# Laying the weight matrices of a two-block transformer kernel out by chunk, so that each load is contiguous in HBM

## The chip, the cores and the metric

One core of one Trainium2 chip. The metric is device time in microseconds (us) of one launch. TensorE (PE) multiplies, VectorE (DVE), ScalarE (ACT) and GpSimd (POOL) work elementwise, and SyncE (SP) does nothing here but issue DMAs. Two engines issue DMAs: SP issues nearly all of them, ACT a handful.

## The reference

Two blocks follow one another on a sequence of 512 tokens of width 1024, in fp32; all weights are read once.

```
mod = silu(c) @ w_ada + b_ada                      # 1024 x 6144; six vectors of 1024
h = rmsnorm(x) * (1 + sc1) + sh1
proj = h @ w_in                                    # 1024 x 2760
dilated attention (8 heads) + indexed sparse attention (8 heads) -> mixed
x = x + ga1 * (mixed @ w_out)
x = x + ga2 * ((silu(gate) * up) @ w_down)         # gate, up = h2 @ w_gu, 1024 x 5632
x = rmsnorm(x)
# second block
mod = silu(c_2) @ mod_w_2 + mod_b_2                # 1024 x 3072
u = (rmsnorm(x) * (1 + scale) + shift) @ w_in_2    # 1024 x 5120
31-tap depthwise convolution, layernorm, silu, @ pw2_w_2; a linear recurrence beside it
x = x + (1 + gate) * (concat(y_conv, y_lru) @ w_out_2); rmsnorm
```

## The kernel before

Activations stand transposed in SBUF: 128 partitions by 8 slices (k) by 512 tokens. Every fp32 product is made of three products of a rounded part ("hi") and its rest ("lo"): hi by hi, lo by hi, hi by lo.

**Weights** come in chunks of 256 output columns. A chunk is 1024 x 256 values (1 MB) and lands in `w_stage[n % 2]`, 128 partitions by 8 slices by 256 columns. ACT rounds it into `w_hi`, POOL (DVE for the first ones) subtracts into `w_lo`, and PE uses it. SP loads chunk n as soon as `w_lo` of chunk n-2 is made (L474, in `w_dma`). In HBM the matrices stand as the reference has them, row by row, so that a chunk is 1024 pieces of 1 KB. There are 11 chunks of `w_in`, 4 of `w_out`, 22 of `w_gu`, 12 of `w_down`, 20 of `w_in_2`, 4 of `pw2_w_2` and 8 of `w_out_2`.

**Modulation** matrices (`w_ada`, `mod_w_2`) come in 36 chunks of the same size, through L487, L558 and L564 and buffers of their own. The first eight (`ADA_PE`) are multiplied by PE (`ada_rows`, L841) and turned into columns (`ada_turn`, L850); the others by DVE (L2206, L2209).

**The start** is written out by hand. SP issues, in this order: `x` in four parts (L490), two modulation chunks, the first half of `w_in` chunk 0 (L502), `w_in` chunk 1, two more modulation chunks, the other half of chunk 0, four more modulation chunks, and so on. ACT issues four small loads in its own queue: the identity, `c`, `c_2`, and `vrow`, 256 KB of bias and gain vectors (L1382) in 512 pieces of 512 bytes.

PE works strictly in program order. What it does first:

```
for t in range(TT):                       # L866: turn x, slices 0 to 5
pe.wait_ge(s_vec, 16)                     # waits for vrow
                                          # L876: turn vrow; L866 again: slices 6 and 7
pe.wait_ge(s_cact, 1)
ada_rows(0)                               # L841, first modulation chunk
pe.matmul(bank[4][:], ones[:], rstd[:], ...)   # L887
ada_rows(1)                               # L841, second
keep_warm(4, 3); ada_turns(0); keep_warm(14, 3)   # L769, L850
```

`keep_warm` is matmuls whose result nobody reads. Then come, on the first two slices, the first products of `w_in` (`abreast(first, 0, (0, 1))`, L746 to L748), `ada_pair(1)` (modulation chunks three and four, then L850), `abreast` of the second chunk, and so on. The columns that L876 makes of `vrow` are copied by ACT to `vcol` (L1394, L1395); DVE adds them to each modulation vector (L1931).

Of the kernel before, what the change touches and what calls it, by code (L numbers as in the profile page):

```python
# [20 lines left out]
P = 128  # L21
T = 512
TT = T // P
D = 1024
KD = D // P
D_FF = 2816
# [6 lines left out]
NCOL = 256  # L33
# [7 lines left out]
W_IN_COLS = [2304, 2048, 2560, 1536, 1792, 0, 256, 512, 768, 1024, 1280]  # L41
N_IN = len(W_IN_COLS)
C_OUT = N_IN
C_GU = C_OUT + 4
C_DOWN = C_GU + 2 * (D_FF // NCOL)
C_IN2 = C_DOWN + 12
C_LRU = C_IN2 + 20
C_PW2 = C_LRU + 4
C_OUT2 = C_PW2 + 4
# [3 lines left out]
ADA1, ADA2 = 24, 12  # L53
ADA_FIRST, ADA_ATT, ADA_OUT, ADA_LOOP, ADA_DOWN = 8, 16, 20, 24, 35
# [5 lines left out]
ADA_BUF = [0, 2, 5, 7, 1, 4, 6, 8] + [n % 4 for n in range(ADA_ATT - ADA_FIRST)] + [0, 2, 3, 9]  # L60
# [95 lines left out]
def build(nc, a, out):  # L156
    with ExitStack() as ctx:
        offset = [nc.sbuf_base + (-nc.sbuf_base) % 64]

        def fixed(name, shape, dt=F32, at=None):  # L160

            n = 4
            for s in shape[1:]:
                n *= s
            if at is None:
                at = offset[0]
                offset[0] += (n + 63) // 64 * 64
                assert offset[0] <= nc.sbuf_usable_end, (name, offset[0])
            return nc.alloc_sbuf_tensor_at(name, shape, dt, offset=at), at

        def sem(name):
            return ctx.enter_context(nc.semaphore(name))
# [5 lines left out]
        w_stage = [fixed(f"w_stage{b}", [P, KD, NCOL])[0] for b in range(2)]  # L178
# [65 lines left out]
        for b, at in enumerate((at_va, at_ka, at_qb, at_qi, at_score, at_ki, at_pairT, at_qa), start=2):  # L244
            ada_bufs.append(fixed(f"ada_stage{b}", [P, KD, NCOL], at=at)[0])
        ada_stage = [ada_bufs[b] for b in ADA_BUF]
# [9 lines left out]
        ada2_stage, _ = fixed("ada2_stage", [P, KD, NCOL])  # L256
        ada2_acc, _ = fixed("ada2_acc", [P, NCOL])
        late_stage = [ada2_stage] + [fixed(f"late_stage{b}", [P, KD, NCOL], at=(at_hi, at_lo)[b // 2] + (b % 2) * 4 * KD * NCOL)[0]
                                     for b in range(len(ADA_LATE) - 1)]
# [45 lines left out]
        s_stage = [sem(f"w_stage_loaded{b}") for b in range(2)]  # L305
        s_stage0 = sem("first_half_chunk_loaded")
# [7 lines left out]
        s_ada = [sem(f"ada_loaded{b}") for b in range(10)]  # L314
# [4 lines left out]
        s_adaloop = sem("ada_loop_loaded")  # L319
# [125 lines left out]
        def ada_use(c):  # L445

            return ADA_BUF[:c + 1].count(ADA_BUF[c])
# [7 lines left out]
            engine.wait_ge(s_ada[ADA_BUF[c]], 16 * ada_use(c))  # L455


        def w_cols(w, k0, kn, c0):
            return w.rearrange("(k p) c -> p k c", p=P)[:, k0:k0 + kn, bass.ds(c0, NCOL)]


        @block.sync
        def _(sp):
            def w_dma(n, src, half=None):

                b = n % 2 if half is None else half[0]

                if half is None:
                    if n >= 2:
                        sp.wait_ge(s_lo, n - 1)  # L470
                else:
                    sp.wait_ge(s_lo, n - 1)
                kn, cn = src.shape[1], src.shape[2]
                sp.dma_start(w_stage[b][:, 0:kn, 0:cn], src).then_inc(s_stage[b], 16)  # L474

            def ada_dma(c):
                if ada_use(c) > 1:
                    last = max(o for o in range(c) if ADA_BUF[o] == ADA_BUF[c])
                    if last in ADA_PE:
                        sp.wait_ge(s_adadir, ADA_PE.index(last) + 1)  # L480
                    else:
                        sp.wait_ge(s_adaacc, ADA_ORD[last] + 1)
                elif ADA_BUF[c] == 3:
                    sp.wait_ge(s_xt, KD)
                w, j = (a["w_ada"], c) if c < ADA1 else (a["mod_w_2"], c - ADA1)
                src = w.rearrange("(p t) c -> p t c", t=KD)[:, :, j * NCOL:(j + 1) * NCOL]
                sp.dma_start(ada_stage[c][:], src).then_inc(s_ada[ADA_BUF[c]], 16)  # L487

            for t in range(TT):
                sp.dma_start(x_nat[:, t, :], a["x"][t * P:(t + 1) * P, :]).then_inc(s_x[t], 16)  # L490

            def w_in_dma(n):
                c0 = W_IN_COLS[n]
                cn = min(NCOL, a["w_in"].shape[1] - c0)
                w_dma(n, a["w_in"].rearrange("(k p) c -> p k c", p=P)[:, :, c0:c0 + cn])

            ada_dma(ADA_PE[0])
            ada_dma(ADA_PE[1])

            def first_chunk_dma(h):  # L500
                ks = slice(h * KD // 2, (h + 1) * KD // 2)
                sp.dma_start(w_stage[0][:, ks, :], a["w_in"].rearrange("(k p) c -> p k c", p=P)[  # L502
                    :, ks, W_IN_COLS[0]:W_IN_COLS[0] + NCOL]).then_inc((s_stage0, s_stage[0])[h], 16)

            first_chunk_dma(0)
            w_in_dma(1)
            ada_dma(ADA_PE[2])
            ada_dma(ADA_PE[3])
            first_chunk_dma(1)
# [12 lines left out]
            for n in range(N_IN - 4):  # L522
                if ADA_FIRST + 4 + n < ADA_ATT:
                    ada_dma(ADA_FIRST + 4 + n)
                if n == 3:
# [2 lines left out]
                    sp.dma_start(wuk[:], a["w_uk"].rearrange("r (g c) -> r g c", g=4)).then_inc(s_late, 16)  # L528
                    sp.dma_start(wuv[:], a["w_uv"].rearrange("h r d -> r h d")).then_inc(s_late, 16)
                w_in_dma(n + 4)  # L530
            w_dma(C_OUT, w_cols(a["w_out"], 0, KD, 0))
            w_dma(C_OUT + 1, w_cols(a["w_out"], 0, KD, NCOL))
            w_dma(C_OUT + 2, w_cols(a["w_out"], 0, KD, 2 * NCOL))
            w_dma(C_OUT + 3, w_cols(a["w_out"], 0, KD, 3 * NCOL))
            sp.wait_ge(s_pv, 2 * N_A)
            for c in range(ADA_ATT, ADA_OUT):
                ada_dma(c)
# [1 line left out]
            def stream(n0, steps, srcs, first=0):  # L539

                per = len(srcs)
                with sp.Fori(first, first + steps) as j:
                    for q, src in enumerate(srcs):
                        w_dma(j * per + (n0 + q - first * per), src(j), half=((n0 + q) % 2,))


            sp.wait_ge(s_res, 1)
            w_dma(C_GU, w_cols(a["w_gu"], 0, KD, 0))
            w_dma(C_GU + 1, w_cols(a["w_gu"], 0, KD, D_FF))
            sp.wait_ge(s_adaacc, ADA_DVE)  # L550
            sp.dma_start(ada2_stage[:], a["mod_w_2"].rearrange("(p t) c -> p t c", t=KD)[
                :, :, (ADA_LOOP - ADA1) * NCOL:(ADA_LOOP - ADA1 + 1) * NCOL]).then_inc(s_adaloop, 16)
            sp.wait_ge(s_bias, 1)
            with sp.Fori(3, KF // 2 + 2) as j:
                w_dma(j * 2 + (C_GU - 4), w_cols(a["w_gu"], 0, KD, j * NCOL - 2 * NCOL), half=(C_GU % 2,))
                w_dma(j * 2 + (C_GU - 3), w_cols(a["w_gu"], 0, KD, j * NCOL + (D_FF - 2 * NCOL)), half=((C_GU + 1) % 2,))
                sp.wait_ge(s_adaacc, j + (ADA_DVE - 2))
                sp.dma_start(ada2_stage[:], a["mod_w_2"].rearrange("(p t) c -> p t c", t=KD)[  # L558
                    :, :, bass.ds(j * NCOL + (ADA_LOOP - ADA1 - 2) * NCOL, NCOL)]).then_inc(s_adaloop, 16)

            def late_dma(b):
                c = ADA_LATE[b]
                w, j = (a["w_ada"], c) if c < ADA1 else (a["mod_w_2"], c - ADA1)
                sp.dma_start(late_stage[b][:], w.rearrange("(p t) c -> p t c", t=KD)[:, :, j * NCOL:(j + 1) * NCOL]).then_inc(  # L564
                    s_ada[b], 16)

            for n in range(12):
                k0, kn = ((0, 8), (8, 8), (16, 6))[n % 3]
                w_dma(C_DOWN + n, w_cols(a["w_down"], k0, kn, n // 3 * NCOL))
                if n == 0:  # L570
                    sp.wait_ge(s_adaacc, ADA_ORD[ADA_LATE[0]])
                    late_dma(0)
                if n == 2:
                    sp.wait_ge(s_wused, C_DOWN)
                if n in (2, 3):
                    late_dma(2 * n - 3)
                    late_dma(2 * n - 2)
            w_dma(C_IN2, w_cols(a["w_in_2"], 0, KD, D))
            w_dma(C_IN2 + 1, w_cols(a["w_in_2"], 0, KD, 0))
            sp.wait_ge(s_adaacc, len(ADA_ORD) + 1)  # L580
            stream(C_IN2 + 2, 3, [lambda j: w_cols(a["w_in_2"], 0, KD, j * NCOL + (D - NCOL)),
                                  lambda j: w_cols(a["w_in_2"], 0, KD, j * NCOL - NCOL)], first=2)
            for g in range(2):
                if g == 0:
                    sp.wait_ge(s_res, 2 * KD)
                sp.dma_start((wr, wi)[g][:], a[("wr_2", "wi_2")[g]].rearrange("h d e -> d h e")).then_inc(s_lruw, 16)
            for part in (3, 4, 2):
                n0 = C_IN2 + 8 + 4 * (3, 4, 2).index(part)
                stream(n0, 2, [lambda j, q=q, part=part: w_cols(a["w_in_2"], 0, KD, j * 2 * NCOL + part * D + q * NCOL)
                               for q in range(2)])  # L590
            stream(C_LRU, 2, [lambda j, q=q: w_cols(a["w_out_2"], KD, KD, j * 2 * NCOL + q * NCOL) for q in range(2)])
            stream(C_PW2, 2, [lambda j, q=q: w_cols(a["pw2_w_2"], 0, KD, j * 2 * NCOL + q * NCOL) for q in range(2)])
            stream(C_OUT2, 2, [lambda j, q=q: w_cols(a["w_out_2"], 0, KD, j * 2 * NCOL + q * NCOL) for q in range(2)])

            for half, t in ((0, 0), (0, 1), (0, 2), (0, 3), (1, 0), (1, 2)):
                cols = slice(half * D // 2, (half + 1) * D // 2)
# [1896 lines left out]
```

## Time and profile before

| | us |
|---|---|
| median of three runs | 1047.95 (1047.81 to 1049.33) |
| the profiled execution's span | 1046.3 |
| PE busy | 1029.7 |
| DVE, POOL, ACT busy | 669.7, 471.6, 431.6 |
| PE's wait for its first data | 4.8 |

The profile gives the span of one execution, from its first instruction to its last; no other time of that execution is shown. The median of the runs lies 1.65 us above the span. An engine's busy time is the sum of its instructions, and DMA share is the mean busy share of the 16 DMA engines. A row that names a releaser says what ended an engine's wait.

### The profile page before, as it was taken

The page shows a single profiled execution, that of the slowest core. Times are in us where ns is not written, and L with a number is a line of the kernel's source. Part 1 is how long each engine was busy: PE and PEld are TensorE (multiplying, and loading weights), DVE is VectorE, ACT ScalarE, POOL GpSimd, SP SyncE. Part 2 cuts the span into 40 slices and gives each one's busy share as a digit, 9 for nine tenths or more (in the row PEclk, how much of TensorE's full clock was granted, in tenths as well). Part 3 has the DMA queues.
Part 4 walks back from the last instruction along what each step waited for, and adds up shares of the span by engine and source line. Part 5 has one row for each costly group of instructions (what it writes and reads, how often), then busy time and mean ns, then how long its engine had stood idle before and what let it go on. Part 6 is the DMA issues. An engine that isn't in the chain of part 4 may idle for free.

```text
span 1046.3 us, 13984 instructions
## 1 busy us (share of the span) xinstructions
PE 1029.7 (98%) x5166; PEld 831.4 (79%) x5166; DVE 669.7 (64%) x1268; ACT 431.6 (41%) x601; POOL 471.6 (45%) x176
## 2 busy tenths in 40 slices
PE   7999999999999999999999999999999999999997
PEld 5687786767888888888888888888887778888886
DVE  6367997786776223323248223599999999886322
ACT  4244325884353212112233322444536888362232
POOL 0034342692424543534533544356774766733440
PEclk9999999999999999999999999999999999999999
DMA  9994231140326344454365233225231223323212
GB/s 327 349 285 136 81 111 51 43 163 1 121 81 201 120 137 144 130 175 136 120 203 180 83 108 111 81 81 155 86 96 65 81 81 97 105 81 113 89 41 80
DMA packets 127250, 128.90 MB, mean 123 GB/s; under 512 B 3552, under 2 KB 125280, under 8 KB 127200
## 3 DMA queue, kind: packets, MB, share of 16 engines
q1 hardware_dynamic: 125952, 127.38, 37.6%
q10 hardware_dynamic: 1248, 0.86, 0.3%
q8 instruction: 31, 0.51, 0.2%
q14 instruction: 19, 0.16, 0.0%
HBM read 126.13 MB, written 2.10 MB: 123 GB/s over the span
## 4 chain that ended last, share of the span: by engine, by line
PE 90%; DVE 3%; DMA 2%; ACT 1%; SPq 1%; POOL 1%; issue 1%; DVEq 0%; ACTq 0%
PE bank L734 22%; PE bank L736 22%; PE bank L735 22%; PE bank L1079 2%; PE bank L1050 2%; PE bank L922 2%; PE bank L1306 1%; PE bank L1308 1%; PE bank L1307 1%; PE bank L746 1%; PE bank L748 1%; PE bank L747 1%; DMA ada_stage<-in_w_ada 1%; PE bank L1264 1%; POOL w_lo L608 1%; PE bank L940 1%
## 5 line engine op out<-in xcount | busy, mean ns | idle before, releaser
L608 POOL TENSOR_TENSOR w_lo<-w_stage,w_hi 128x2048 fp32r<-128x2048 f32 x77 | 368.3, 4783 | 478.6 <-ACT w_hi L1377 478.6
L734 PE MATMUL bank<-act_hi,w_hi 128*128 128x512 f32 x832 | 329.2, 396 | 0.0
L736 PE MATMUL bank<-act_hi,w_lo 128*128 128x512 f32 x832 | 323.9, 389 | 0.0
L735 PE MATMUL bank<-act_lo,w_hi 128*128 128x512 f32 x832 | 323.8, 389 | 0.0
L1377 ACT ACTIVATE w_hi<-w_stage 128x2048 fp32r<-128x2048 f32 x78 | 149.3, 1914 | 234.5 <-PE bank L736 210.4
L734 PEld LDWEIGHTS bank<-act_hi,w_hi 128*128 128x128 f32 x832 | 156.3, 188 | 37.8 <-issue 4.9
L735 PEld LDWEIGHTS bank<-act_lo,w_hi 128*128 128x128 f32 x832 | 156.3, 188 | 32.9 <-issue 1.4
L736 PEld LDWEIGHTS bank<-act_hi,w_lo 128*128 128x128 f32 x832 | 156.2, 188 | 32.8
L2309 DVE SCALAR_TENSOR_TENSOR bank<-v_pad,vcol,bank 128x512 f32<-128x512 f32 x208 | 138.2, 746 | 0.0
L736 PE MATMUL bank<-ff_hi,w_lo 128*128 128x512 f32 x176 | 69.3, 394 | 0.0
L734 PE MATMUL bank<-ff_hi,w_hi 128*128 128x512 f32 x176 | 69.0, 392 | 0.0
L735 PE MATMUL bank<-ff_lo,w_hi 128*128 128x512 f32 x176 | 68.8, 391 | 0.0
L2206 DVE TENSOR_SCALAR bank<-ada_stage,c_act 128x256 f32<-128x256 f32 x11 | 5.4, 487 | 80.8 <-PE bank L1186 80.8
L2215 DVE TENSOR_TENSOR tmp<-bank,tmp 128x512 f32<-128x512 f32 x22 | 15.1, 691 | 61.5 <-PE bank L736 61.5
L1626 ACT ACTIVATE tmp<-bank 128x512 f32<-128x512 f32 x20 | 12.0, 599 | 84.5 <-PE bank L736 84.5
L735 PEld LDWEIGHTS bank<-ff_lo,w_hi 128*128 128x128 f32 x176 | 33.1, 188 | 7.4
L734 PEld LDWEIGHTS bank<-ff_hi,w_hi 128*128 128x128 f32 x176 | 33.1, 188 | 7.0
L736 PEld LDWEIGHTS bank<-ff_hi,w_lo 128*128 128x128 f32 x176 | 33.1, 188 | 6.9
L2139 DVE SCALAR_TENSOR_TENSOR xT<-bank,mod,xT 128x512 f32<-128x512 f32 x8 | 6.0, 750 | 45.3 <-PE bank L736 45.3
L2209 DVE SCALAR_TENSOR_TENSOR bank<-ada_stage,c_act,bank 128x256 f32<-128x256 f32 x66 | 32.3, 490 | 2.3
L2144 DVE SCALAR_TENSOR_TENSOR xT<-bank,scale,xT 128x512 f32<-128x512 f32 x16 | 11.8, 747 | 26.1 <-PE bank L736 26.0
L673 POOL TENSOR_TENSOR comb<-table,work 128x256 f32<-128x256 f32 (+2 forms) x24 | 24.4, 1048 | 6.7 <-DVE negmax L2009 6.2
(352 smaller groups left out, 1659.7 us busy)
## 6 DMA issues: line engine op xcount, KB each, us to landing
w_stage<-in_w_in SPq DMA_DIRECT2D x29, 1024.0 KB, 5.2
w_stage<-in_w_gu SPq DMA_DIRECT2D x22, 1024.0 KB, 5.2
ada_stage<-in_w_ada SPq DMA_DIRECT2D x20, 1024.0 KB, 11.6
w_stage<-in_w_out SPq DMA_DIRECT2D x12, 1024.0 KB, 5.1
ada_stage<-in_mod_w SPq DMA_DIRECT2D x12, 1024.0 KB, 5.4
w_stage<-in_w_down SPq DMA_DIRECT2D x8, 1024.0 KB, 5.1
late_stage<-in_w_ada SPq DMA_DIRECT2D x4, 1024.0 KB, 9.5
w_stage<-in_pw_w SPq DMA_DIRECT2D x4, 1024.0 KB, 5.1
```

Source lines behind the costliest of these rows:

```text
L608: nc.gpsimd.tensor_tensor(w_lo[b][:], w_stage[b][:], w_hi[b][:].bitcast(F32), ALU.subtract).then_inc(s_lo, 1)
L673: nc.gpsimd.tensor_tensor(comb[s % 4][:, 0:n], t, held, ALU.add).then_inc(s_comb, 1)
L734: pe.matmul(dst, wh, rhs_hi(k), start=(first and k == 0), stop=False)
L735: pe.matmul(dst, wh, rhs_lo(k), start=False, stop=False)
L736: mm = pe.matmul(dst, wl, rhs_hi(k), start=False, stop=(last and k == n_k - 1))
L922: pe.matmul(bank[SCORE_BANK[v % 2][m]][:, 0:n], q[half, p, qs], k[half, p, 0:n], start=True, stop=True).then_inc(s_s, 1)
L1050: mm = pe.transpose(bank[TURN_BANK[m]][:, kb * P:(kb + 1) * P], probs[s % 4][:, kb * P:(kb + 1) * P], ident[:])
L1079: mm = pe.matmul(o[HD * m:HD * m + HD, qs], vals, pairT[v % 3][:, m, kb, :], start=(kb == 0), stop=(kb == i))
L1377: nc.scalar.activation(w_hi[b][:], w_stage[b][:], ACT.Copy).then_inc(s_hi, 1)
L2209: V.scalar_tensor_tensor(ada2_acc[:] if t == KD - 1 else bank[4][:, 0:NCOL], src, w, bank[4][:, 0:NCOL], ALU.mult, ALU.add).then_inc(s_ada ...
L2215: V.tensor_tensor(tmp[2 + m][:], bank[2 + m][:], tmp[m][:], ALU.mult).then_inc(s_up, 1)
L2309: V.scalar_tensor_tensor(conv[:, k, :] if tap == CONV - 1 else acc, src, w, acc, ALU.mult, ALU.add).then_inc(s_conv, 1)
```

## The change

The host stores each matrix as chunks: `w_in`, `w_out`, `w_gu`, `w_down`, `w_in_2`, `pw2_w_2` and `w_out_2` as (chunk, partition, k slice, 256 columns), `w_ada` and `mod_w_2` likewise. A whole chunk is then 8 KB in one piece for each partition. `w_in`'s last chunk, 200 columns wide before, is padded to 256. Half a chunk is a piece of 4 KB, the third part of a `w_down` chunk (6 slices) one of 6 KB. Number, order, waits, semaphores and issuing engine of all DMAs stay; ACT's four loads are not changed, nor are `x`, `wr_2`, `wi_2`, `w_uk`, `w_uv`.

```diff
-        def w_cols(w, k0, kn, c0):
-            return w.rearrange("(k p) c -> p k c", p=P)[:, k0:k0 + kn, bass.ds(c0, NCOL)]
+        def w_chunk(w, n, k0=0, kn=KD):
+
+            if isinstance(n, int):
+                return w[n, :, k0:k0 + kn, :]
+            return w[bass.ds(n, 1), :, k0:k0 + kn, :].rearrange("o p k c -> (o p) k c")
...
-                src = w.rearrange("(p t) c -> p t c", t=KD)[:, :, j * NCOL:(j + 1) * NCOL]
-                sp.dma_start(ada_stage[c][:], src).then_inc(s_ada[ADA_BUF[c]], 16)
+                sp.dma_start(ada_stage[c][:], w_chunk(w, j)).then_inc(s_ada[ADA_BUF[c]], 16)
...
-                c0 = W_IN_COLS[n]
-                cn = min(NCOL, a["w_in"].shape[1] - c0)
-                w_dma(n, a["w_in"].rearrange("(k p) c -> p k c", p=P)[:, :, c0:c0 + cn])
+                w_dma(n, w_chunk(a["w_in"], W_IN_COLS[n] // NCOL))
...
-                sp.dma_start(w_stage[0][:, ks, :], a["w_in"].rearrange("(k p) c -> p k c", p=P)[
-                    :, ks, W_IN_COLS[0]:W_IN_COLS[0] + NCOL]).then_inc((s_stage0, s_stage[0])[h], 16)
+                sp.dma_start(w_stage[0][:, ks, :], w_chunk(a["w_in"], W_IN_COLS[0] // NCOL, h * KD // 2, KD // 2)).then_inc((s_stage0, s_stage[0])[h], 16)
...
-                w_dma(C_DOWN + n, w_cols(a["w_down"], k0, kn, n // 3 * NCOL))
+                w_dma(C_DOWN + n, w_chunk(a["w_down"], n // 3, k0, kn))
...
+    for name in ("w_in", "w_out", "w_gu", "w_down", "w_in_2", "pw2_w_2", "w_out_2"):
+        w = tables[name]
+        w = np.pad(w, ((0, 0), (0, -w.shape[1] % NCOL)))
+        tables[name] = np.ascontiguousarray(w.reshape(-1, P, w.shape[1] // NCOL, NCOL).transpose(2, 1, 0, 3))
+    for name in ("w_ada", "mod_w_2"):
+        w = tables[name]
+        tables[name] = np.ascontiguousarray(w.reshape(P, KD, -1, NCOL).transpose(2, 0, 1, 3))
```

The other loads are rewritten in the same way.

## Rows read from the trace of the kernel before

**Rows 1.** The page: span, busy times, DMA packets

```profile
span 1046.3 us, 13984 instructions
...
PE 1029.7 (98%) x5166; PEld 831.4 (79%) x5166; DVE 669.7 (64%) x1268; ACT 431.6 (41%) x601; POOL 471.6 (45%) x176
...
DMA packets 127250, 128.90 MB, mean 123 GB/s; under 512 B 3552, under 2 KB 125280, under 8 KB 127200
```

**Rows 2.** Waits of PE, whole span: us in total, times, longest

```profile
PE bank L866 <- DMA ident_sb<-in_ident: 4.8, 1, 4.8
PE bank L841 <- DMA ada_stage<-in_w_ada: 2.3, 3, 0.9
PE bank L1050 <- ACT pairT L1571: 0.7, 2, 0.4
...
PE bank L876 <- DMA vrow<-in_vecs: 0.4, 1, 0.4
...
PE bank L829 <- DVE tmp L1835: 0.2, 1, 0.2
```

**Rows 3.** Chain that ended last, its first 70 us: start, us, what

```profile
13.87 13.43 DMA ada_stage<-in_w_ada
```

**Rows 4.** Timeline of PE, 10.6 to 29.5 us

```profile
10.64 0.62 PE L876 MATMUL bank<-ident_sb,vrow 128*128 128x128 f32 x4 [0.44 <-DMA vrow<-in_vecs]
11.10 1.04 PE L866 MATMUL bank<-ident_sb,x_nat 128*128 128x128 f32 x8
12.63 1.04 PE L841 MATMUL bank<-ada_stage,c_act 128*1 128x256 f32 x16 [0.49 <-DMA ada_stage<-in_w_ada]
13.60 1.13 PE L887 MATMUL bank<-rstd,ones 128*128 128x512 f32 x2
15.64 1.04 PE L841 MATMUL bank<-ada_stage,c_act 128*1 128x256 f32 x16 [0.91 <-DMA ada_stage<-in_w_ada]
...
18.42 3.37 PE L769 MATMUL bank<-ones 128*128 128x128 f32 x28
...
25.38 1.04 PE L841 MATMUL bank<-ada_stage,c_act 128*1 128x256 f32 x16
27.35 1.04 PE L841 MATMUL bank<-ada_stage,c_act 128*1 128x256 f32 x16 [0.93 <-DMA ada_stage<-in_w_ada]
28.32 1.18 PE L850 MATMUL bank<-fourths,ada_acc 128*128 128x1 f32 x8
```

**Rows 5.** Timeline, all engines: the first product and a later pair

```profile
22.44 0.47 PE L746 MATMUL bank<-act_hi,w_hi 128*128 128x512 f32 x1 [0.65 <-DVE act_lo L1948]
...
35.30 1.91 PE L841 MATMUL bank<-ada_stage,c_act 128*1 128x256 f32 x32
...
37.13 1.18 PE L850 MATMUL bank<-fourths,ada_acc 128*128 128x1 f32 x8
```

**Rows 6.** Stretches: us, busy of PE, PEld, DVE, ACT, POOL, PEclk, DMA share, GB/s

```profile
5.00:7.00 2.00, 2.00 (x11) 1.98 (x11) 2.00 (x3) 0.00 (x0) 0.00 (x0) 1.00 1.06 405
11.00:15.00 4.00, 3.23 (x29) 1.53 (x27) 2.72 (x8) 1.84 (x5) 0.00 (x0) 1.00 1.09 348
```

**Rows 7.** DMA queues, 7 to 7.9 us: q1 SP's, q10 ACT's; packets, MB

```profile
q1 hardware_dynamic: 82, 0.31, 86.5%
q10 hardware_dynamic: 82, 0.04, 15.2%
```

**Rows 8.** DMA queues, 7.9 to 9.5 us

```profile
q1 hardware_dynamic: 353, 0.36, 67.9%
q10 hardware_dynamic: 357, 0.18, 40.6%
```

**Rows 9.** DMA queues, 7.9 to 10.7 us

```profile
q10 hardware_dynamic: 430, 0.21, 27.5%
```

**Rows 10.** Stretches, L866 alone: us, busy PE, PEld, PEclk, DMA share, GB/s

```profile
4.70:10.30 5.60, 5.38 (x24) 4.71 (x24) 1.00 1.06 373
10.90:12.20 1.30, 1.04 (x8) 0.90 (x8) 1.00 1.08 345
```

More of the change, by code:

```diff
@@ L530, in _ @@
                 w_in_dma(n + 4)
[L531 to L534, printed above, removed]
+            w_dma(C_OUT, w_chunk(a["w_out"], 0))
+            w_dma(C_OUT + 1, w_chunk(a["w_out"], 1))
+            w_dma(C_OUT + 2, w_chunk(a["w_out"], 2))
+            w_dma(C_OUT + 3, w_chunk(a["w_out"], 3))
             sp.wait_ge(s_pv, 2 * N_A)
@@ L547, in _ @@
             sp.wait_ge(s_res, 1)
-            w_dma(C_GU, w_cols(a["w_gu"], 0, KD, 0))
-            w_dma(C_GU + 1, w_cols(a["w_gu"], 0, KD, D_FF))
+            w_dma(C_GU, w_chunk(a["w_gu"], 0))
+            w_dma(C_GU + 1, w_chunk(a["w_gu"], D_FF // NCOL))
             sp.wait_ge(s_adaacc, ADA_DVE)
-            sp.dma_start(ada2_stage[:], a["mod_w_2"].rearrange("(p t) c -> p t c", t=KD)[
-                :, :, (ADA_LOOP - ADA1) * NCOL:(ADA_LOOP - ADA1 + 1) * NCOL]).then_inc(s_adaloop, 16)
+            sp.dma_start(ada2_stage[:], w_chunk(a["mod_w_2"], ADA_LOOP - ADA1)).then_inc(s_adaloop, 16)
             sp.wait_ge(s_bias, 1)
             with sp.Fori(3, KF // 2 + 2) as j:
-                w_dma(j * 2 + (C_GU - 4), w_cols(a["w_gu"], 0, KD, j * NCOL - 2 * NCOL), half=(C_GU % 2,))
-                w_dma(j * 2 + (C_GU - 3), w_cols(a["w_gu"], 0, KD, j * NCOL + (D_FF - 2 * NCOL)), half=((C_GU + 1) % 2,))
+                w_dma(j * 2 + (C_GU - 4), w_chunk(a["w_gu"], j - 2), half=(C_GU % 2,))
+                w_dma(j * 2 + (C_GU - 3), w_chunk(a["w_gu"], j + (D_FF // NCOL - 2)), half=((C_GU + 1) % 2,))
                 sp.wait_ge(s_adaacc, j + (ADA_DVE - 2))
-                sp.dma_start(ada2_stage[:], a["mod_w_2"].rearrange("(p t) c -> p t c", t=KD)[
-                    :, :, bass.ds(j * NCOL + (ADA_LOOP - ADA1 - 2) * NCOL, NCOL)]).then_inc(s_adaloop, 16)
+                sp.dma_start(ada2_stage[:], w_chunk(a["mod_w_2"], j + (ADA_LOOP - ADA1 - 2))).then_inc(s_adaloop, 16)
             def late_dma(b):
@@ L563, in late_dma @@
                 w, j = (a["w_ada"], c) if c < ADA1 else (a["mod_w_2"], c - ADA1)
-                sp.dma_start(late_stage[b][:], w.rearrange("(p t) c -> p t c", t=KD)[:, :, j * NCOL:(j + 1) * NCOL]).then_inc(
+                sp.dma_start(late_stage[b][:], w_chunk(w, j)).then_inc(
                     s_ada[b], 16)
@@ L577, in _ @@
                     late_dma(2 * n - 2)
-            w_dma(C_IN2, w_cols(a["w_in_2"], 0, KD, D))
-            w_dma(C_IN2 + 1, w_cols(a["w_in_2"], 0, KD, 0))
+            w_dma(C_IN2, w_chunk(a["w_in_2"], D // NCOL))
+            w_dma(C_IN2 + 1, w_chunk(a["w_in_2"], 0))
             sp.wait_ge(s_adaacc, len(ADA_ORD) + 1)
-            stream(C_IN2 + 2, 3, [lambda j: w_cols(a["w_in_2"], 0, KD, j * NCOL + (D - NCOL)),
-                                  lambda j: w_cols(a["w_in_2"], 0, KD, j * NCOL - NCOL)], first=2)
+            stream(C_IN2 + 2, 3, [lambda j: w_chunk(a["w_in_2"], j + (D // NCOL - 1)),
+                                  lambda j: w_chunk(a["w_in_2"], j - 1)], first=2)
             for g in range(2):
@@ L588, in _ @@
                 n0 = C_IN2 + 8 + 4 * (3, 4, 2).index(part)
-                stream(n0, 2, [lambda j, q=q, part=part: w_cols(a["w_in_2"], 0, KD, j * 2 * NCOL + part * D + q * NCOL)
+                stream(n0, 2, [lambda j, q=q, part=part: w_chunk(a["w_in_2"], j * 2 + (part * D // NCOL + q))
                                for q in range(2)])
-            stream(C_LRU, 2, [lambda j, q=q: w_cols(a["w_out_2"], KD, KD, j * 2 * NCOL + q * NCOL) for q in range(2)])
-            stream(C_PW2, 2, [lambda j, q=q: w_cols(a["pw2_w_2"], 0, KD, j * 2 * NCOL + q * NCOL) for q in range(2)])
-            stream(C_OUT2, 2, [lambda j, q=q: w_cols(a["w_out_2"], 0, KD, j * 2 * NCOL + q * NCOL) for q in range(2)])
+            stream(C_LRU, 2, [lambda j, q=q: w_chunk(a["w_out_2"], j * 2 + q, KD) for q in range(2)])
+            stream(C_PW2, 2, [lambda j, q=q: w_chunk(a["pw2_w_2"], j * 2 + q) for q in range(2)])
+            stream(C_OUT2, 2, [lambda j, q=q: w_chunk(a["w_out_2"], j * 2 + q) for q in range(2)])
             for half, t in ((0, 0), (0, 1), (0, 2), (0, 3), (1, 0), (1, 2)):
```

## The prediction

> **What bounds the kernel now.** I read the page first. PE is busy for 98% of the span [rows 1], so a faster load pays only where PE stands still for one. The waits of PE come next [rows 2]: 4.8 us for the identity before any work, a load that is not changed; 2.3 us in three waits for modulation chunks; 0.4 us for `vrow`; and, after 30 us, waits for DVE and ACT of 0.2 to 0.7 us, none for a DMA. So all that is loaded after the start arrives in time already, and the change can only act before PE's last DMA wait, which ends at 27.35 us [rows 4].
>
> The chain of the start shows the fourth modulation chunk, issued at 13.87 and landed 13.43 us later, at 27.3 [rows 3]: it stood in a full queue. The timeline of PE [rows 4] shows what hangs on what: L876 at 10.64 when `vrow` is there, the first modulation product at 12.63 and the second at 15.64 when their chunks are there, the first product of `w_in` at 22.44 [rows 5], then the third and fourth modulation products at 25.38 and 27.35, and L850 at 28.32. From there PE has no gap that a load ends, so **the change is worth what it does to the start of that L850**.
>
> **What each piece costs.** The queue moves 405 GB/s while `x` comes in pieces of 4 KB, and 348 GB/s in the pieces of 1 KB of the chunks [rows 6]. Per DMA engine (a sixteenth) a piece of 1 KB takes 1024 x 16 / 348 = 47 ns, one of 4 KB 162 ns at most, and about 154 when ACT's small pieces between them are taken out (an estimate). That is 36 ns for each further KB, so I estimate a piece of 8 KB at 300 ns (154 x 2 less some 8 for one start saved). A 1 MB chunk is 8 pieces per engine: 2.4 us in place of 3.0. That it will be one piece: of 127,250 packets 1,920 have from 2 to 8 KB [rows 1], and these are the 512 of `x`, 1,024 of the output, 128 each of `dist` and `maskA`, and 128 of `w_uk`, whose destination has three dimensions just as the new loads' have. It was merged into one run for each partition; so will they be.
>
> **First term, a gain: the modulation chunks.** The second lands after two chunks of the new kind: 2 x 0.57 = 1.1 us earlier. The fourth has 5.5 MB of changed pieces ahead of it, itself included: 5.5 x 0.57 = 3.1 us earlier, at 24.2. With nothing else changed the second product starts at 14.5, the first `w_in` product ends 1.1 us earlier, and the two next modulation products run back to back as in the later pair (35.30 to 37.13, 1.83 us until L850 [rows 5]): from 24.24 to 26.1, which is 2.2 us before 28.32.
>
> **Second term, a loss: `vrow`.** ACT's queue shares the 16 engines with SP's. From 7 to 7.9 us, beside 4 KB pieces, SP's queue had 82 packets and ACT's 82 [rows 7]; from 7.9 to 9.5, beside 1 KB pieces, 353 and 357 [rows 8]. The engines take one packet of each in turn, whatever their sizes. From 7.9 us on 430 of ACT's are left [rows 9], 16 of them completions: 414, or 26 per engine. Before, a pair took 1.6 x 16 / 355 = 72 ns, so 26 took 1.9 us, to 9.8, and PE started L876 at 10.64 (0.8 us later).
>
> After the change each of the 26 waits for a long packet: 8 of the first modulation chunk, 8 of the second, 8 of the half chunk (4 KB) and 2 of `w_in` chunk 1. That is 18 x 300 + 8 x 154 + 26 x 27 (a 512 byte packet: the rest of the 72 ns pair, 25 to 31) = 5.4 + 1.2 + 0.7 = 7.3 us. The last leaves at 15.2, and L876 starts at 16.0, 5.4 us late. The Trainium skill, in DMA: Bandwidth & Descriptors, section Queues, rings and completion order, says that an engine goes round the queues packet by packet, and that a packet may hold some 9 to 17 descriptors; this trace agrees with the turns and shows one piece to each (82 to 82, 353 to 357).
>
> Queued behind the wait on `vrow` on PE, in its order: L876 (0.35 until L866), L866 (0.9), the first modulation product (0.97), L887 (0.85), then the second modulation product: 3.1 us [rows 4], so 19.1 in place of 15.64, 3.5 us late; its chunk has long landed. `vcol` waits too: ACT's and DVE's copies of the turned `vrow` took until 13.8, 3.1 us after L876 began, so they set the same 19.1. From the second product to the first `w_in` product lie 6.8 us through ACT, L850, DVE and `keep_warm` (15.64 to 22.44), and that work is the same: 25.9. That product and its eleven fellows end at 28.85 (22.44 to 25.38 before). The third and fourth chunks are there, so 1.83 us later, at 30.7, L850 starts: **2.4 us later than before**. With its chunk there, the fourth product would have let L850 start at 25.38 + 1.83 = 27.2 before: these 1.1 us of waiting are what the loss eats first.
>
> **Third term: the clock.** PE is idle from 10.3 to 16.0, where it was idle for 0.4 us. The view prints a granted clock of 1.00 throughout, but L866's weight loads took 4.71 us for 24, 196 ns each, right after the idle start, and 0.90 for 8, 112 ns each, from 10.9 on [rows 10]: the first at 1.2 GHz and the second at 2.4, I read. PE had stood idle for 4.8 us before the first; now it will for 5.7. If the clock falls, what follows 16.0 runs slowly until it rises. From below: 0, it does not fall. From above: it took until about 10.7 to rise, 5.9 us of work; half of that lost is 2.9 us. Between: the twelve transposes at 84 ns more, 1.0 us, and half as much again on the first modulation product, 0.5 us. I take 1.5, since the nearest row (an idle of 4.8 us, then slow work) says that it falls. Past 19 us the slow clock has the 0.65 us of slack before L746 to eat [rows 5], and the 28 `keep_warm` matmuls (3.37 us) stand in the way.
>
> The Trainium skill (TensorE: Matmul & The Clock Gate, section The HAM clock gate) has the throttled clock as the default that activity lifts. It bears on the third term alone: by it the fall is the rule after such a pause. Without the fall the sum is 2.4.
>
> **Other edits, at nothing.** SP's own issuing (up to 13.4 us per load in the queue [rows 3], fewer pieces to write) hides behind the transfers; if it did not, the loads would only come early, which PE after 30 us does not wait for. The padded chunk is 0.2 MB more, 0.5 us in a queue whose lateness no PE wait shows after 27.35. Beyond the start no load stands on ACT's queue until the end. The late chain through DVE into L829 costs PE 0.2 us [rows 2] and hangs on no chunk's rate.
>
> **Sum.** 2.4 + 1.5 = 3.9 us against the span of 1046.3: 1050.2. The median is 1.65 above the span, so 1051.8.
>
> **Rivals.**
> - *Starved, but the clock holds.* For it: the printed clock of 1.00. Against: rows 10. 1047.95 + 2.4 = 1050.35.
> - *ACT's queue is not starved* (the turn goes by bytes, or small pieces go first). This is the other side: the first term alone, -2.2 us, 1045.75. The point where it decides: the loss must first fill the 1.1 us of waiting in front of the fourth product, so with `vrow`'s start at L876 before 13.7 the kernel is not slower. That is 26 pairs in 5.0 us, 190 ns a pair, long packets of about 4.5 KB. Against it: rows 7 and 8, the same turn at two sizes.
> - *The 8 KB runs are cut into pieces of 4 KB.* Then 26 x (154 + 27) = 4.7 us, L876 at 13.4, the second product at 16.5, 0.8 late, the fourth product no longer waits: -0.3 us, 1047.6. For it: no load in this trace has a piece over 4 KB.
> - *No merging*: pieces of 1 KB as now, 1047.95. The count of rows 1 speaks against it.
>
> **Chances.** Starved with a fall of the clock 0.45 (1051.8, from 1050.8 to 1053.3), starved without 0.28, not starved 0.12, cut 0.09, not merged or something else that comes to no change 0.06. The range of 8 in 10 leaves out the unstarved case and a little above the full price of the clock: 1047.4 to 1053.7. A measurement of this kernel tells 0.2%, 2.1 us, from no change. Slower by more: 0.45 and two thirds of 0.28, 0.63. Within: the rest of 0.28, the cut and unmerged cases and a third of the unstarved, 0.28. Faster: 0.09.
>
> **What the profile after would show.** ACT's and SP's packets still one to one, SP's at 8 KB; GB/s above 405 from 8 us on; L876 at 16.0 with a DMA wait of some 5.5 us; L841 waiting for no DMA; the transposes after L876 near 196 ns; L850's second group at 30.7 or up to 3 us later; and all after it shifted by a constant. Wrong would be: `vrow` before 13.7, or a PE wait for a load after 30 us.

## The result, and the profile after

The changed kernel takes 1052.78 us (median of four runs, 1052.62 to 1054.55); the kernel before takes 1047.93 (median of four). The ratio is 1.0048, with a 95% interval of 1.0034 to 1.0063: 4.85 us slower. The profiled execution's span is 1050.8 against 1046.3.

The page of the changed kernel, its DMA lines:

```profile
span 1050.8 us, 13984 instructions
...
DMA packets 23570, 129.13 MB, mean 123 GB/s; under 512 B 3552, under 2 KB 6496, under 8 KB 9184
...
q1 hardware_dynamic: 22272, 127.61, 33.5%
```

The same line of the kernel before (packets, MB, share of the 16 engines):

```profile
q1 hardware_dynamic: 125952, 127.38, 37.6%
```

Beside [rows 1]: the layout did what it says. There are 23,570 packets in place of 127,250, the runs were merged, and SP's loads keep the DMA engines busy for 33.5% of the span in place of 37.6%. Yet the kernel is slower. The waits of PE over the whole span (us in total, times, longest) say where:

```profile
PE bank L873 <- DMA vrow<-in_vecs: 5.4, 1, 5.4
PE bank L863 <- DMA ident_sb<-in_ident: 4.9, 1, 4.9
PE bank L1047 <- ACT pairT L1568: 0.7, 2, 0.4
PE bank L743 <- DVE act_lo L1945: 0.6, 1, 0.6
PE bank L1032 <- DVE vb L2054: 0.2, 1, 0.2
```

Beside [rows 2]: the waits for modulation chunks (2.3 us) are gone, and the wait for `vrow` has grown from 0.4 to 5.4. Line numbers are three lower in this kernel: L873 is L876 of before, L863 is L866, L838 is L841, L847 is L850.

The timeline of PE in the changed kernel, 15 to 34 us, answers to [rows 4] and [rows 5]:

```profile
15.73 1.02 PE L873 MATMUL bank<-ident_sb,vrow 128*128 128x128 f32 x4 [5.37 <-DMA vrow<-in_vecs]
16.54 1.92 PE L863 MATMUL bank<-ident_sb,x_nat 128*128 128x128 f32 x8
18.38 1.88 PE L838 MATMUL bank<-ada_stage,c_act 128*1 128x256 f32 x16
20.20 1.59 PE L884 MATMUL bank<-rstd,ones 128*128 128x512 f32 x2
21.72 1.04 PE L838 MATMUL bank<-ada_stage,c_act 128*1 128x256 f32 x16
...
28.52 0.47 PE L743 MATMUL bank<-act_hi,w_hi 128*128 128x512 f32 x1 [0.65 <-DVE act_lo L1945]
...
31.46 1.91 PE L838 MATMUL bank<-ada_stage,c_act 128*1 128x256 f32 x32
33.30 1.18 PE L847 MATMUL bank<-fourths,ada_acc 128*128 128x1 f32 x8
```

`vrow` is turned 5.1 us late, the second modulation product starts 6.1 late (21.72 for 15.64), the second group of L847 5.0 late (33.30 for 28.32). The same eight transposes that took 1.04 us before take 1.92. The stretches of the changed kernel (us, busy of PE, PEld, DVE, ACT, POOL, granted clock, DMA share, GB/s) show why:

```profile
5.00:14.00 9.00, 5.35 (x24) 4.62 (x24) 7.41 (x16) 3.57 (x7) 0.00 (x0) 1.00 1.03 406
14.30:20.90 6.60, 5.17 (x29) 3.23 (x30) 0.96 (x2) 1.49 (x4) 0.00 (x0) 0.50 1.03 423
21.10:30.00 8.90, 8.25 (x69) 6.54 (x68) 5.00 (x8) 4.47 (x5) 0.00 (x0) 1.00 1.02 418
```

The granted clock was 0.50 from 14.3 to 20.9, which is 1.2 GHz, after PE had stood still since 10.3. The 1.00 of the first row needs care. The view prints 1.00 up to the trace's first record of the clock, and that record is a rise at 10.9 us. The 24 transposes before it took some 223 ns each (5.35 us), as slow as work at 0.50; at the high clock it is 130 (1.04 us for eight). So before its fall the clock had been high only from 10.9 to 14.3, all of it inside the pause.

And the queues of the changed kernel from 8 to 15 us (packets, MB; q1 is SP's, q10 ACT's):

```profile
q1 hardware_dynamic: 444, 2.66, 92.6%
q10 hardware_dynamic: 430, 0.22, 10.9%
```

Beside [rows 8]: still one packet of each in turn, only that 444 of SP's are now 2.66 MB.

### The profile page after: what moved, and what is told of

Same layout as the page of the kernel before. It is cut to its first block, busy times and chain, and to the rows that moved or that the text cites. A ratio compares the mean times of both kernels' runs of the same rounds, so it can differ in the third digit from the quotient of the medians.

```text
span 1050.8 us, 13984 instructions
## 1 busy us (share of the span) xinstructions
PE 1031.8 (98%) x5166; PEld 832.8 (79%) x5166; DVE 671.2 (64%) x1268; ACT 431.6 (41%) x601; POOL 471.5 (45%) x176
## 2 busy tenths in 40 slices
DMA packets 23570, 129.13 MB, mean 123 GB/s; under 512 B 3552, under 2 KB 6496, under 8 KB 9184
## 3 DMA queue, kind: packets, MB, share of 16 engines
q1 hardware_dynamic: 22272, 127.61, 33.5%
## 4 chain that ended last, share of the span: by engine, by line
PE 95%; DMA 1%; ACT 1%; POOL 1%; DVE 1%; issue 0%; ACTq 0%; DVEq 0%
PE bank L731 23%; PE bank L733 23%; PE bank L732 23%; PE bank L1076 2%; PE bank L1047 2%; PE bank L919 2%; PE bank L743 1%; PE bank L1303 1%; PE bank L1305 1%; PE bank L1304 1%; PE bank L745 1%; PE bank L744 1%; DMA vrow<-in_vecs 1%; PE bank L1261 1%; POOL w_lo L605 1%; PE bank L937 1%
## 5 line engine op out<-in xcount | busy, mean ns | idle before, releaser
L2141 DVE SCALAR_TENSOR_TENSOR xT<-bank,scale,xT 128x512 f32<-128x512 f32 x16 | 11.8, 746 | 26.1 <-PE bank L733 26.0
## 6 DMA issues: line engine op xcount, KB each, us to landing
ada_stage<-in_w_ada SPq DMA_DIRECT2D x20, 1024.0 KB, 10.7
```

## Experiments

Two causes had to be told apart: the turns between the two queues, and the clock that falls in the pause. The main rival was that the contiguous loads cost something by themselves, at the start or later. The 95% intervals below are some 1 us to either side, so a difference of less than that between two medians is not told by them alone. The medians below stand beside a kernel before of 1047.92, 1047.91 and 1047.88 us in the three groups of runs.

**Fewer pieces for `vrow`, in both kernels.** The host stores the vectors so that `vrow` is 2 KB in one piece per partition.

```diff
-            nc.scalar.dma_start(vrow[:], a["vecs"].rearrange("(q r) c -> r q c", r=P)).then_inc(s_vec, 16)
+            nc.scalar.dma_start(vrow[:], a["vecs"].rearrange("r (q c) -> r q c", q=4)).then_inc(s_vec, 16)
...
-    tables["vecs"] = vecs
+    tables["vecs"] = np.ascontiguousarray(vecs.reshape(4, P, P).transpose(1, 0, 2)).reshape(P, 4 * P)
```

On the changed kernel:

> The changed kernel, and the host also lays the bias and gain vectors out so that vrow is 128 pieces of 2 KB instead of 512 of 512 bytes. Theory (an engine takes one piece of each queue in turn, so vrow's price is its number of pieces times SP's piece): 8 turns per DMA engine instead of 32, most of them beside the 4 KB pieces of x; vrow is there when x is turned, PE starts on it near 10.4 us, PE's wait for it is under 0.5 us, the clock stays high, the second modulation product starts at 14.5 and the second group of L847 near 26.1 (33.3 in the changed kernel); span near 1043.8, time near 1045.4. Rival (the long loads take the engines by bytes, or hurt elsewhere): vrow lands near 15.7 again and the time stays near 1052.8.

Measured: 1045.37 us, ratio to the kernel before 0.9979 (0.9970 to 0.9988). Its timeline of PE:

```profile
10.59 0.62 PE L873 MATMUL bank<-ident_sb,vrow 128*128 128x128 f32 x4 [0.60 <-DMA vrow<-in_vecs]
...
14.36 1.04 PE L838 MATMUL bank<-ada_stage,c_act 128*1 128x256 f32 x16 [0.25 <-DMA ada_stage<-in_w_ada]
...
25.93 1.18 PE L847 MATMUL bank<-fourths,ada_acc 128*128 128x1 f32 x8
```

The loss is gone, and the gain of the faster modulation chunks stands there as the prediction's first term had it (second modulation product at 14.5, second group of L847 at 26.1). On the kernel before:

> The kernel before with vrow in 128 pieces of 2 KB. Theory: PE waits for modulation chunks there, vrow had 2 us to spare, so the time stays within 0.3 us of 1047.9. Rival (vrow's own shape is what pays, whatever the weights' layout): about as much faster than the kernel before as the other run with the wide vrow.

Measured: 1047.60 us, ratio 0.9998 (0.9989 to 1.0007). The shape of `vrow` is worth nothing that can be told while the weights come in pieces of 1 KB: it is the two together that matter.

**`vrow` in SP's own queue, in its 512 pieces.** ACT's load of it is taken out, and SP issues it behind `x`.

```diff
             for t in range(TT):
                 sp.dma_start(x_nat[:, t, :], a["x"][t * P:(t + 1) * P, :]).then_inc(s_x[t], 16)
 
+            sp.dma_start(vrow[:], a["vecs"].rearrange("(q r) c -> r q c", r=P)).then_inc(s_vec, 16)
```

> The changed kernel, with vrow in its 512 pieces of 512 bytes as ever, but issued by SP between x and the first modulation chunk instead of by ACT. Theory (only the turns between the two queues made vrow late): in SP's queue its 32 pieces per DMA engine follow one another at about 31 to 35 ns, 1.1 us after x is through at 7.9; it is there before x is turned, PE's wait for it is under 0.5 us, the second modulation product starts at 14.5 to 14.9, the second group of L847 near 26.3, time near 1045.7, like the run with the wide vrow. Rival (pieces of 512 bytes in the middle of the stream are what is slow): vrow after 12 us and a time above 1047.9.

Measured: 1045.76 us, ratio 0.9980 (0.9971 to 0.9989). From its timeline of PE:

```profile
10.32 0.97 PE L875 MATMUL bank<-ident_sb,vrow 128*128 128x128 f32 x4
...
26.48 1.18 PE L849 MATMUL bank<-fourths,ada_acc 128*128 128x1 f32 x8
```

PE waits for no `vrow` at all. Small pieces are not slow; taking turns with long ones is.

**Shorter pieces for `w_ada` and `w_in`.** The host leaves a gap of 256 bytes behind each 4, 2 or 1 KB of a partition's chunk, so that runs are not merged across it. All else is the changed kernel. The kernel with 4 KB has `PIECES = 2`, the others 4 and 8.

```diff
+        def cut(t, ks=slice(0, KD)):
+            return t[:, ks, :].rearrange("p (g k) c -> p g (k c)", k=KD // PIECES)
...
+        def w_cut(w, n, h=0, halves=1):
+            g = slice(h * PIECES // halves, (h + 1) * PIECES // halves)
+            return w[n, :, g, 0:KD // PIECES * NCOL]
...
+                    sp.dma_start(cut(ada_stage[c]), w_cut(w, j)).then_inc(s_ada[ADA_BUF[c]], 16)
...
+        tables[name] = np.pad(w.reshape(w.shape[0], P, 2, -1), ((0, 0), (0, 0), (0, 0), (0, 64)))
```

> The changed kernel, but w_ada and w_in are stored with a gap of 256 bytes behind each 4 KB, so that their chunks load as two pieces of 4 KB per partition instead of one of 8 KB. Theory (one piece each in turn): 26 turns at 154 + 27 ns, vrow lands near 13.3 us instead of 15.7, the clock does not fall, the second modulation product starts near 16.4, the second group of L847 near 27.9, span near 1045.5, time near 1047.2. Rival (turns by bytes, or the delay comes of the contiguity itself): time near 1052.8.

Measured: 1050.52 us, ratio 1.0024 (1.0015 to 1.0033). The expected time is missed by 3.3 us, though `vrow` is turned where it was expected. Its timeline of PE, and its stretches:

```profile
13.45 1.02 PE L889 MATMUL bank<-ident_sb,vrow 128*128 128x128 f32 x4 [3.50 <-DMA vrow<-in_vecs]
14.27 1.91 PE L879 MATMUL bank<-ident_sb,x_nat 128*128 128x128 f32 x8
...
19.18 1.04 PE L854 MATMUL bank<-ada_stage,c_act 128*1 128x256 f32 x16
...
30.75 1.18 PE L863 MATMUL bank<-fourths,ada_acc 128*128 128x1 f32 x8
```

```profile
5.00:11.50 6.50, 4.50 (x24) 3.96 (x24) 6.09 (x13) 3.44 (x7) 0.00 (x0) 1.00 1.03 395
11.80:18.40 6.60, 4.95 (x29) 3.20 (x30) 2.25 (x5) 1.44 (x4) 0.00 (x0) 0.50 1.03 409
18.60:25.00 6.40, 6.40 (x61) 5.16 (x60) 2.69 (x5) 2.85 (x5) 0.00 (x0) 1.00 1.03 410
```

What was wrong is the expectation that the clock would not fall. PE had been idle since 9.95, the trace records the fall at 11.5 us, and the clock was 0.50 from there until 18.4.

> The changed kernel with a gap of 256 bytes behind each 2 KB of w_ada and w_in, so that their chunks load in four pieces of 2 KB per partition. Theory (one piece each in turn): 26 turns at about 84 + 27 ns, L873 near 11.6 us, too short an idle for the clock to fall (it fell after an idle of 1.8 us with pieces of 4 KB, so this is near the edge), the second modulation product near 15.0, the second group of L847 near 26.6, span near 1044.2, time near 1045.9, faster than the kernel before. Rival (only the layout as such slows the start, in proportion to nothing): above 1047.9.

Measured: 1047.60 us, ratio 0.9995 (0.9986 to 1.0004), no difference that can be told. `vrow` is turned at 12.04:

```profile
12.04 0.62 PE L889 MATMUL bank<-ident_sb,vrow 128*128 128x128 f32 x4 [1.63 <-DMA vrow<-in_vecs]
...
27.04 1.18 PE L863 MATMUL bank<-fourths,ada_acc 128*128 128x1 f32 x8
```

The eleven runs of this kernel lie in two groups, five from 1046.12 to 1046.66 and five from 1047.60 to 1047.73 (one took 1049.14). The profiled one (span 1044.5, clock 1.00 after the pause) belongs to the first, near the expected 1045.9. A clock that falls in some executions and not in others would do that, and the mean granted clock of each whole execution speaks for it: 0.998 to 0.999 in the first five, 0.997 in every one of the second five, beside 0.995 to 0.997 with pieces of 4 KB. No profile of an execution of the second group was taken, so where the clock fell in them is not shown. The one of 1049.14 has 0.999; its delay is something else.

> The changed kernel with a gap of 256 bytes behind each 1 KB of w_ada and w_in, so that these load in pieces of 1 KB as before, while w_gu, w_down, w_out, w_in_2, pw2_w_2, w_out_2 and mod_w_2 keep their contiguous chunks. Theory (all of the change's effect sits in the start): vrow lands at 10.6, waits for modulation chunks as before, second group of L847 near 28.3, time within 0.4 us of 1047.9. Rival (the contiguous loads of the later stages cost or gain something): any other time.

Measured: 1047.80 us, ratio 0.9999 (0.9990 to 1.0008); `vrow` is turned at 10.87 and the second group of L863 (L850 of before) starts at 28.40. The 82 chunks that this kernel still loads in long pieces, all those outside `w_ada` and `w_in`, change the time by nothing that can be told, which is less than some 1 us. The rival that they cost the 4.85 us later on falls.

**The clock by itself.** More `keep_warm` matmuls stand in front of PE's wait for `vrow` and write a bank that is overwritten next. Loads are those of the changed kernel.

```diff
+            keep_warm(34, 6)
             pe.wait_ge(s_vec, 16)
```

> The changed kernel with 34 more keep_warm matmuls on PE, in front of its wait for vrow, into the bank that vrow's turning overwrites. Theory (the starved wait and the fallen clock add up): the wait ends at 15.7 all the same, the granted clock stays 1.00 through it, the second modulation product starts near 18.9 instead of 21.7, the second group of L847 near 30.5 instead of 33.3, span near 1048.2, time near 1050.1. Rival (the clock costs nothing, the whole delay is the wait): time 1052.8.

Measured: 1051.67 us, ratio 1.0038 (1.0024 to 1.0051). The clock held, but this run missed its number, because the matmuls themselves became the delay:

```profile
9.79 7.76 PE L766 MATMUL bank<-ones 128*128 128x128 f32 x68
17.39 0.56 PE L874 MATMUL bank<-ident_sb,vrow 128*128 128x128 f32 x4
...
20.79 1.04 PE L838 MATMUL bank<-ada_stage,c_act 128*1 128x256 f32 x16
```

Each is two instructions of some 0.11 us, and they ran until 17.4, 1.7 us past the time at which `vrow` had been turned without them. From L874 to the second modulation product it is 3.40 us at the high clock, where the changed kernel took 5.99. With 25:

> The changed kernel with 25 more keep_warm matmuls in front of PE's wait for vrow, which take 5.6 us by the 0.112 us that each of their two halves took in the run with 34 (those overshot the wait by 1.6 us). Theory: they end near 15.4, before vrow lands; granted clock 1.00 all through the start; L873 near 15.8, the second modulation product 3.4 later at 19.2, the second group of L847 near 30.8, span near 1048.4, time near 1050.2. What is left over the kernel before (2.3) is the starved wait alone, what goes (2.6) is the clock. Rival (the clock costs nothing): 1052.8.

Measured: 1050.49 us, ratio 1.0024 (1.0014 to 1.0034). Its timeline of PE, and one stretch:

```profile
16.11 0.62 PE L874 MATMUL bank<-ident_sb,vrow 128*128 128x128 f32 x4 [0.17 <-DMA vrow<-in_vecs]
...
19.56 1.04 PE L838 MATMUL bank<-ada_stage,c_act 128*1 128x256 f32 x16
```

```profile
11.80:18.40 6.60, 6.43 (x66) 5.52 (x64) 2.25 (x5) 1.17 (x4) 0.00 (x0) 1.00 1.03 414
```

So of the 4.85 us, 2.3 were the clock (1052.78 less 1050.49), and 2.6 are left for the wait. The mean granted clock of whole executions says that the profiles are not exceptions: 0.994 to 0.996 in all four of the changed kernel, 0.998 to 0.999 in all with 25 or 34 of these matmuls in the pause.

The same with 14 of them on the kernel with pieces of 4 KB:

> The kernel with the 4 KB pieces, and 14 more keep_warm matmuls (3.1 us) in front of the wait for vrow. Theory: L889 at 13.45 as without them, granted clock 1.00, second modulation product 3.4 later at 16.9 (19.2 without them), second group of L863 near 28.4 (30.75), span near 1046.0, time near 1047.7 (1050.5): with pieces of 4 KB the wait alone costs nothing, and the clock was the whole loss. Rival (the 4 KB loads cost something besides the wait): time stays near 1050.5.

Measured: 1048.25 us, ratio 1.0001 (0.9992 to 1.0010); 2.3 us less than without them, and half a microsecond above the expected number. In the profile they overshot the wait by 1.2 us:

```profile
10.95 3.92 PE L782 MATMUL bank<-ones 128*128 128x128 f32 x28
14.71 0.56 PE L890 MATMUL bank<-ident_sb,vrow 128*128 128x128 f32 x4
```

With 4 KB the late `vrow` alone costs nothing that can be told, and the clock was the loss, as far as medians with intervals of 1 us tell it. The fourteen matmuls took 3.92 us, not 3.1, because the first of them still ran at the slow clock of the start: in this trace the first rise comes at 12.3 us. The profiled execution is the slowest of the eleven (1049.08), and its span (1047.2) is only 1.1 below that of the run without them (1048.3) while the medians differ by 2.3, so it is not the typical one.

## Why the prediction was right

**Where the change can act: right.** PE's last wait that hangs on a load is in the start, and with `w_ada` and `w_in` back at 1 KB the time is that of before.

**The first term, a gain of 2.2 us: right**, and hidden in the changed kernel. With the wide `vrow` the second group of L847 starts 2.4 us earlier than before (25.93 for 28.32), and the time is 2.55 us lower. The estimate of 2.4 us for a chunk holds too: 423 GB/s in the stretch from 14.3 to 20.9 is 2.5 us for 1 MB.

**The second term, `vrow`: right in mechanism and size.** 26 turns beside long packets were to bring L876 to 16.0; it came at 15.73. With pieces of 4 KB 13.4 was worked out and 13.45 measured. At the high clock the second product comes 3.40 us after, as the run with 34 `keep_warm` matmuls shows, so at 19.1. The prediction has 19.1 too, but there two errors of 0.3 us cancel: the start was put too late (16.0) and the way from there too short (3.1 us), and that is luck. The 2.4 us that the term gives at L850 would be 2.1 in the time, with the 0.3 us that come back (below); the run with 25 `keep_warm` matmuls is 2.6 above the kernel before. Its profiled execution, which is also its median one, began on its first data 0.5 us later than that of the changed kernel.

**The third term, the clock: right in sign, too small.** 1.5 us were taken between 0 and 2.9. The profile of the changed kernel has 5.99 - 3.40 = 2.6 us of it, the medians 2.3. Beside the run with 34 `keep_warm` matmuls the twelve transposes took 1.3 us more (1.0 in the prediction), the first modulation product 0.8 (0.5), and L884, which the prediction left out and which ran at 1.2 GHz as well, 0.5.

The ground that the prediction gave for the fall does not carry it. Its row (4.8 us of idleness, then slow work [rows 10]) shows no fall: the first record of the clock in the trace of the kernel before is a rise, at 9.9 us, and nothing shows a high clock earlier. That the clock falls in a pause is first shown by the changed kernel, so this step came out right without a row that bears it. The Trainium skill (TensorE: Matmul & The Clock Gate, section The HAM clock gate) has the fall as the rule after a pause; the rows of the changed kernel and of the run with 4 KB agree (0.50 in pauses of 5.4 and 3.5 us).

**The step that was wrong** is small: "The late chain through DVE into L829 costs PE 0.2 us and hangs on no chunk's rate". It does hang on one, and this is the term put at nothing that was not nothing. In the timelines, ACT's rounding of a `w_down` chunk, first of the kernel before, then of the changed one:

```profile
540.19 1.92 ACT L1377 ACTIVATE w_hi<-w_stage 128x2048 fp32r<-128x2048 f32 x1 [11.12 <-DMA w_stage<-in_w_down]
```

```profile
543.41 1.92 ACT L1374 ACTIVATE w_hi<-w_stage 128x2048 fp32r<-128x2048 f32 x1 [9.39 <-DMA w_stage<-in_w_down]
```

PE is 5.0 us late there, but this comes only 3.2 us later. ACT is free sooner for what DVE's chain needs, and PE's wait for DVE at L829 [rows 2] is gone from the waits after. L829 comes in three groups. PE is 4.95 us late at the second (570.13 for 565.18) and 4.63 at the third (575.16 for 570.53), so this gives 0.32 us back. The run with the start at 1 KB shows it apart from the start. PE in the kernel before, then in that run, where L829 is L842:

```profile
565.85 0.61 PE L829 MATMUL bank<-ones,tmp 128*128 128x1 f32 x4 [0.17 <-DVE tmp L1835]
570.53 0.50 PE L829 MATMUL bank<-ones,rstd 128*128 128x1 f32 x4
```

```profile
565.14 0.95 PE L842 MATMUL bank<-ones,tmp 128*128 128x1 f32 x8
570.17 0.50 PE L842 MATMUL bank<-ones,rstd 128*128 128x1 f32 x4
```

From the second group to the third it is 5.35 us in the kernel before, 5.03 in that run and in the changed kernel. With the wide `vrow` and pieces of 1 KB it is 5.15, so by these single traces 0.1 to 0.3 us hang on the chunk's pieces.

The sum by what was measured: 5.0 (2.4 and 2.6) at the second L847, less 0.3, and 0.1 less by the end is the 4.6 by which the span grew (4.56 before it is rounded). The medians differ by 0.3 us more; single executions of one kernel differ by as much and more (1052.62 to 1054.55 here).

**The rivals.** That the 8 KB runs are not merged, or that ACT's queue is not starved, is shown wrong by the packets. The cut into 4 KB was put at -0.3 us; made by hand it is 2.6 slower, since that rival left the clock out. That the clock holds is wrong here.

## What to carry to other kernels

When one queue's loads are made of longer pieces, look for a small load in the other queue at the same time: it pays one long piece for each of its own, so count its pieces per DMA engine, multiply, and see who waits. The remedy is to make that load of fewer pieces, or to put it in the same queue ahead of the long ones: either turned 4.85 us of loss into a gain of 2.1 to 2.6 here. The one with fewer pieces is the version to take (1045.37 us), though 1045.76 is too near to be told from it. And when PE gains a pause, price its slow clock as well as the pause.

## What the runs showed of the hardware that was not expected

The clock fell in a shorter pause than the prediction had weighed. With pieces of 4 KB PE was idle from 9.95 us, the clock fell at 11.5 and rose again at 18.4, and PE had been working again for 5 us by then. The fall cost about as much after 3.5 us of pause as after 5.4: from the turning of `vrow` to the second modulation product it is 5.73 us there and 5.99 in the changed kernel, against 3.40 at the high clock.

The clock can also rise in a pause. In the changed kernel it rose at 10.9 us, when PE had already stopped at 10.3, and fell at 14.3 before PE had done anything. With pieces of 2 KB it rose at 10.9 as well, PE went on at 12.04, and the clock stayed at 1.00. So that profile, with its pause of 1.6 us, does not show that a high clock outlasts a pause of that length.
